# Mixer stage of a two-block transformer kernel: value tiles in halves, gate product in eight pieces, one output block moved

## What is computed

```
u = rmsnorm_2(h, attn_norm_w)
gq, gk, gv, gz, gb, ga, fq, fk, fv, ff = split(u @ w_in)
# gated delta rule, in chunks: M = 16 meta tokens, then 128 and 128
sol = triangular_solve(a_mat + eye, [v * beta, k * (beta * exp(gc))])
v_new = u_c - w_c @ state
o_c = (q_c * exp(g_c)) @ state + qk_c @ v_new
state = state * exp(g_last) + (k_c * exp(g_last - g_c)).T @ v_new
o_gdn = o * rsqrt(mean(o * o) + EPS) * norm_w * silu(gz)
# forgetting attention
p = softmax(causal(q @ k.T * scale + c[q] - c[k]));  o_fox = p @ fv
h = h + concat([o_gdn, o_fox]) @ w_out
h = h + swiglu(rmsnorm_2(h, ffn_norm_w))
```

## Time and profile before

| | us |
|---|---|
| median of 3 runs | 934.2 (932.55 to 935.7) |
| the profiled execution | 935.33 |
| its span in the trace | 933.7 |
| PE busy | 915.9 (98%) |
| DVE busy | 627.7 (67%) |
| ACT busy | 481.6 (52%) |
| granted PE clock, mean | 0.996 of full |

### The profile page before, as it was taken

One profiled execution on the slowest core, in us unless ns is written; L12 is line 12 of the kernel. 1 busy time (PEld: TensorE's weight loads), 2 busy tenths in 40 slices (PEclk: granted clock), 3 DMA queues, 4 the chain that ended last, 5 costly groups with the idle time before them and its releaser, 6 DMA issues.

```text
span 933.7 us, 16660 instructions
## 1 busy us (share of the span) xinstructions
PE 915.9 (98%) x6746; PEld 812.6 (87%) x6746; DVE 627.7 (67%) x962; ACT 481.6 (52%) x845; POOL 98.5 (11%) x107
## 2 busy tenths in 40 slices
PE   8999999999999999999999999999999999999997
PEld 8988778877998999998788789999678899999885
DVE  5974376546896587778874477998665667666543
ACT  6334447436655464565754457665444554445432
POOL 1000031001230000101320003400000011111001
PEclk9999999999999999999999999999999999999999
DMA  9745345555555775332015454432111455555551
GB/s 323 280 161 180 135 151 174 177 180 176 181 189 204 271 259 206 136 136 92 1 57 196 155 184 137 177 136 92 48 47 33 154 203 198 204 181 190 204 193 46
DMA packets 23520, 150.41 MB, mean 161 GB/s; under 512 B 3564, under 2 KB 3848, under 8 KB 6168
## 3 DMA queue, kind: packets, MB, share of 16 engines
q1 hardware_dynamic: 23104, 149.20, 46.3%
q10 hardware_dynamic: 344, 0.18, 0.1%
HBM read 148.30 MB, written 1.05 MB: 160 GB/s over the span
## 4 chain that ended last, share of the span: by engine, by line
PE 81%; DVE 9%; ACT 5%; DMA 2%; issue 2%; POOL 0%; SPq 0%; ACTq 0%; POOLq 0%; DVEq 0%
PE psum L794 77%; DVE ring_parts L2140 4%; DMA ring<-in_weights 2%; ACT high_parts L1688 1%; PE psum L875 1%; ACT R L1877 1%; DVE R L2470 1%; PE psum L1224 1%; DMA h<-in_x 1%; DVE R L2422 1%; PE psum L1569 0%; DVE PTb_parts L2441 0%; DVE PTb L2639 0%; ACT Pf L2060 0%; PE psum L1494 0%
## 5 line engine op out<-in xcount | busy, mean ns | idle before, releaser
L2140 DVE TENSOR_TENSOR ring_parts<-ring,high_parts 128x1024 fp32r<-128x1024 f32 (+1 forms) x272 | 330.1, 1253 | 150.8 <-ACT high_parts L1688 149.6
L1688 ACT CAST high_parts<-ring 128x1024 fp32r<-128x1024 f32 x268 | 268.2, 1051 | 183.0 <-PE psum L794 141.4
L794 PE MATMUL psum<-xT_parts,high_parts 128*128 128x256 f32 (+1 forms) x1024 | 228.3, 284 | 1.5 <-DVE ring_parts L2140 0.7
L794 PE MATMUL psum<-xT_parts,ring_parts 128*128 128x256 f32 (+1 forms) x704 | 197.5, 281 | 0.0
L794 PEld LDWEIGHTS psum<-xT_parts,high_parts 128*128 128x128 f32 x1024 | 172.7, 189 | 3.9 <-issue 1.8
L794 PE MATMUL psum<-high_parts,R_parts 128*128 128x512 f32 (+1 forms) x528 | 164.8, 386 | 0.0
L794 PE MATMUL psum<-R_parts,high_parts 128*128 128x256 f32 x832 | 156.0, 277 | 0.0
L794 PE MATMUL psum<-high_parts,xT_parts 128*128 128x512 f32 x480 | 154.2, 397 | 0.0
L794 PEld LDWEIGHTS psum<-xT_parts,ring_parts 128*128 128x128 f32 x704 | 132.4, 188 | 0.1
L794 PEld LDWEIGHTS psum<-R_parts,high_parts 128*128 128x128 f32 x832 | 130.5, 188 | 0.0
L794 PEld LDWEIGHTS psum<-high_parts,R_parts 128*128 128x128 f32 (+1 forms) x528 | 98.7, 188 | 20.5
(11 more groups left out here) (365 smaller groups left out, 1050.3 us busy)
## 6 DMA issues: line engine op xcount, KB each, us to landing
ring<-in_weights SPq DMA_DIRECT2D x135, 1024.0 KB, 5.0
h<-in_x SPq DMA_DIRECT2D x4, 256.0 KB, 4.5
ring<-in_weights SPq DMA_DIRECT2D x4, 256.0 KB, 5.8
ring<-in_weights SPq DMA_DIRECT2D x2, 512.0 KB, 7.6
G<-in_gains SPq DMA_DIRECT2D x2, 512.0 KB, 6.9
out<-xn SPq DMA_DIRECT2D x2, 512.0 KB, 2.6
R<-in_ret_tabs SPq DMA_DIRECT2D x1, 768.0 KB, 14.5
G<-in_p_t SPq DMA_DIRECT2D x1, 512.0 KB, 6.6
```

The costliest lines, as they stand in the source:

```text
L794: return pe.matmul(out, lhsT, rhs, start=first, stop=last, skip_group_check=True)
L1688: act.copy(as_r(hi), value).then_inc(sem("units_high"), 1)
L2140: return dve.tensor_tensor(as_r(value), value, value_of(hi), ALU.subtract)
```

## The change

It rewrites the list, and the two helpers that cut a tile. Value tile 2 is made in two halves too (`fvh` 2, `fv` 2), with its second half behind Q 2; tile 3's first half moves behind kv 1 and its second half behind kv 0. The gate product was four entries (two halves of k by two token blocks) of 12 matmuls, three of them in levels 1, 2 and 4 and the last one behind Vo 0. It is now eight entries (four quarters of k by two token blocks) of 6 matmuls, seven of them in levels 1 to 5. The output block `mo` 0, 0 moves from behind Vn 2 to ahead of it. The sums and their matmuls are the same.

```diff
-    order += [("fv", 1), ("Q", 1), ("fv", 2), ("Qm", 1), ("Q", 2), ("fvh", 3), ("Qm", 2), ("kv", 1), ("fv", 3), ("kv", 2),
-              ("Fs", 0), ("kv", 0)]
+    order += [("fv", 1), ("Q", 1), ("fvh", 2), ("Qm", 1), ("Q", 2), ("fv", 2), ("Qm", 2), ("kv", 1), ("fvh", 3), ("kv", 2),
+              ("Fs", 0), ("kv", 0), ("fv", 3)]
     beside = {1: ([("vT", 1), ("vT", 2), ("vT", 0), ("Fn", 0)], [("Ft", 0), ("gz", 0, 0)]),
-              2: ([("Fo", 0)], [("Fs", 1), ("gz", 0, 1)]),
-              3: ([("Fn", 1)], [("Ft", 1)]),
-              4: ([("Fo", 1)], [("Fs", 2), ("gz", 1, 0)]),
-              5: ([("Fn", 2)], [("Ft", 2)]),
+              2: ([("Fo", 0), ("gz", 0, 1)], [("Fs", 1), ("gz", 1, 0)]),
+              3: ([("Fn", 1)], [("gz", 1, 1), ("Ft", 1)]),
+              4: ([("Fo", 1), ("gz", 2, 0)], [("Fs", 2), ("gz", 2, 1)]),
+              5: ([("Fn", 2)], [("gz", 3, 0), ("Ft", 2)]),
               6: ([("Fo", 2)], [("Fs", 3)])}
...
-    order += [("W", 1), ("W", 2), ("Fn", 3), ("Vn", 0), ("Ft", 3), ("Vo", 0), ("gz", 1, 1), ("Vn", 1), ("Fo", 3), ("Vo", 1),
-              ("Vg", 1), ("Vn", 2), ("mo", 0, 0), ("Vo", 2), ("Vg", 2), ("H", 0), ("mo", 0, 1), ("mo", 1, 0), ("mo", 1, 1),
+    order += [("W", 1), ("W", 2), ("Fn", 3), ("Vn", 0), ("Ft", 3), ("Vo", 0), ("gz", 3, 1), ("Vn", 1), ("Fo", 3), ("Vo", 1),
+              ("Vg", 1), ("mo", 0, 0), ("Vn", 2), ("Vo", 2), ("Vg", 2), ("H", 0), ("mo", 0, 1), ("mo", 1, 0), ("mo", 1, 1),
               ("H", 1)]
...
-            def rows_input(name, half, n, chunks):
+            def rows_input(name, quarter, n, chunks):
-                if n == 0:
+                if n == 0 and quarter % 2 == 0:
                     unit[name] = next_unit(4)
...
-                for k in range(4):
-                    ins = parts3(product, bank[0:m, :], x_src(4 * half + k, c0, m), w(k, slice(0, 512)),
-                                 half == 0 and k == 0, half == 1 and k == 3)
-                if half:
+                for k in (2 * quarter, 2 * quarter + 1):
+                    ins = parts3(product, bank[0:m, :], x_src(k, c0, m), w(k % 4, slice(0, 512)), k == 0, k == KD - 1)
+                if quarter == 3:
                     main.full(ins, (name, n))
...
-                    channels_input(kind, *key, 4 if (kind, key) == ("fv", [3]) else 0)
+                    channels_input(kind, *key, 4 if kind == "fv" and key[0] > 1 else 0)
...
-                elif kind == "gz" and key[0]:
+                elif kind == "gz" and key[0] == 3:
```

More of the change, by code:

```diff
@@ L1475, in channels_input @@
             def channels_input(name, j, k0=0, k1=KD):
-                if j % 2 == 0:
+                if j % 2 == 0 and k0 == 0:
                     unit[name] = next_unit(KD)
@@ L1502, in rows_input @@
                 c0, m = chunks[n]
-                bank = main.at((name, n)) if half else main.open(pe, (name, n))
-                for k in range(4):
-                    ins = parts3(product, bank[0:m, :], x_src(4 * half + k, c0, m), w(k, slice(0, 512)),
-                                 half == 0 and k == 0, half == 1 and k == 3)
-                if half:
+                bank = main.at((name, n)) if quarter else main.open(pe, (name, n))
+                for k in (2 * quarter, 2 * quarter + 1):
+                    ins = parts3(product, bank[0:m, :], x_src(k, c0, m), w(k % 4, slice(0, 512)), k == 0, k == KD - 1)
+                if quarter == 3:
                     main.full(ins, (name, n))
```

## The result

The changed kernel takes **941.8 us** (median of ten executions, 936.9 to 943.3), the kernel before 933.05 (ten, 932.2 to 937.1): the ratio is 1.0075, with an interval of 1.0058 to 1.0091. By the ratio it is slower by 7 us (5.4 to 8.5), by the medians by 8.8. The forecast was 936.1 with a range up to 938.6 and "within 0.3%" as the likeliest outcome: wrong in both. The profiled execution of after took 941.5 us with a span of 939.9, 6.2 more than before's 933.7.

The account below looks back on a forecast made before the run. The prediction took TensorE (PE), busy 98% of the span, as the bound, leaving only its pauses and clock to gain. A + B2 (B1 within it) + C = +1.9 on 934.2 gave 936.1 us, range 932.0 to 938.6.

Parts of the forecast that it names:

- within 0.3%: Whole kernel: a time that measurement can't tell from no change, 931.4 to 937.0 us; chance 0.65.
- Term A: Values stage: transposes start 1.2 us later behind a 2.75 us pause, at half clock; +1.0 us, ends 0 and +1.35.
- The prediction's own sign of being wrong: Values stage: the forecast is wrong if the value transposes start before 657.3, or level 4's corrections start with their matmuls.
- rival 1: Value transposes: the clock holds there, the rest as forecast, 935.1 us; chance 0.20.
- Term B1: Levels 1 to 3: gate pieces cut waits from 1.2 to about 0.65 us; -0.55 us, ends -1.2 and +0.3.
- Term B2: Levels 4 and 5: two splits delay the corrections, PE idles 2.15 us; +0.9 us with Term B1 counted in.
- The second fall of the clock: Rival: the clock falls again in level 5's 2.15 us pause, costing 1.7 us, 937.8 us; chance 0.20.
- Term C: Output block: the wait moves from Vn 2 to Vo 2, 0.92 us there; 0.0 us, ends -0.9 and +0.3.
- Sum: Step adding 1.0 + 0.9 + 0.0 = +1.9 us to the median of 934.2, giving 936.1 us.

Follow-up runs that it names:

- e15: The changed kernel with three float32 products instead of two in spread_roots(6), same kernel as e9, one profiled execution: 934.9 us.
- e8: The changed kernel with four float32 products instead of two in spread_roots(6), as a control: 942.35 us (one execution).
- e9: The changed kernel with three float32 products instead of two in spread_roots(6): 942.6 us, ratio 1.0084.
- e13: The changed kernel unaltered, run again for one profile: 939.0 us.
- e10: The changed kernel with the output block back behind Vn 2 (value halves and gate pieces only): 937.65 us, ratio 1.0032.
- e7: The kernel before with the output block's move alone and three float32 products instead of two in spread_roots(6): 934.5 us, ratio 1.0012.
- e4: The changed kernel with unread float32 matmuls inserted ahead of SwiGLU gate and up units, at twenty breaks: 945.5 us (one execution).
- e3: The kernel before with the output block's move ahead of Vn 2 alone: 938.5 us, ratio 1.004.
- e11: The changed kernel with the last half of value tile 3 back ahead of Fs 0 and kv 0: 942.7 us (one execution).
- e6: The kernel before with three float32 products instead of two in spread_roots(6): 939.4 us, ratio 1.0065.
- e12: The changed kernel with gate pieces shifted later, so one DVE split in level 4 instead of two: 940.5 us (one execution).
- e16: The changed kernel with three float32 products instead of two in spread_roots(6), same kernel as e15, one profiled execution: 938.3 us.
- e14: The changed kernel unaltered, same as e13, run again for one profile: 946.5 us.

## Why the prediction was wrong

**Term A (+1.0): right for the profiled execution.** Its chain came out as written. ACT, after: the chunk-0 rows and behind them the cast of the last value half; DVE, after: the split and the copies.
```profile
653.53 1.09 ACT L2021 ACTIVATE R<-psum,small 16x128 f32<-16x128 f32 x4
654.53 1.03 ACT L1687 CAST high_parts<-ring 128x1024 fp32r<-128x1024 f32 x1
```
```profile
655.59 1.23 DVE L2139 TENSOR_TENSOR ring_parts<-ring,high_parts 128x1024 fp32r<-128x1024 f32 x1 [2.06 <-ACT high_parts L1687]
```
The pause was forecast at 2.75 us and is 2.88; the half clock at the transposes came. From the mark to the gate block are 36.20 us before (662.22 - 626.02) and 37.09 after (662.10 - 625.01): +0.89. The prediction's own sign of being wrong, transposes before 657.3, has to be read from that mark too: they start at 657.29, but after is 1.01 us ahead, so they come 0.99 later than before. The pause is a matter of the order, the half clock of the execution: e15 has the same pause (2.88 us ahead of 657.26) and a clock of 1.00 from 656 to 664 us, where after has 0.79. That is what rival 1 said of the clock, and there it came.

**Term B1 (-0.55): right mechanism, undersized.** Fo 1 starts 1.11 us earlier than before (681.41 against 682.52), so levels 1 to 3 give 0.99 back. Of the waits that I had left there (0.35 in level 2, 0.15 to 0.2 at Fs 1, 0.1 in level 3) two of 0.17 us stood.

**Term B2 (+0.9): right place and releaser, oversized.** The resumption in level 5 is at 67.51 us from the mark (692.52) against 66.46 (692.48): +1.05, of which A holds 0.89, so B2 is +0.16. The corrections of level 4 were forecast 1.65 us late from two splits; with A taken off they came 0.9 late (685.45 against 684.69, and 1.01 - 0.89 for mark and A). B1's larger gain took up 0.4 of the difference, and ACT's cast began 0.6 us behind the piece's first matmul (683.23 and 682.64) and not 0.9, which is the rest.

**The second fall of the clock: a rival (0.20) that came.** It was priced at 1.7; from the mark to the value product behind the levels after needs 89.99 us and before 87.92, so the part behind level 5 lost 2.07 - 1.05 = 1.0. This too is a draw: e8, e9 and e13 have the same pause of 1.96 or 1.97 us there and a clock of 1.00 from 690 to 704 us.

**Term C (0.0): right in the mixer.** The wait of 0.90 moved from Vn 2 to Vo 2 and is 0.68 (forecast 0.92): 2.07 became 1.89 us at H 0, -0.2.

So the mixer's sum came out at +1.9 us, as forecast, but by luck: 0.9 + 0.2 + 1.0 - 0.2, where a fall of the clock that the forecast left out makes up for what B2 had too much.

**The step that failed** is the one in "Sum": it adds the terms of the mixer to the old time and takes every stage behind for unchanged, because its instructions are. The long stream took 5.5 us more for the same instructions at the same clock, which is neither a term, nor in a rival's price, nor in the range. The trace of before would have warned me: it has streams of the same matmuls at 117.8 ns (20.9 to 54.6 us) and at 113.3 (247.9 to 283.1 us), and its last stream changed from one to the other at `spread_roots(6)`. The two paces were there to be read; I looked at stretches of the mixer only, because PE had no pause behind it.

The medians are 8.8 us apart and the profiles 6.2, because before's profiled execution lies 2.3 us above its median of ten and after's 0.3 below its own. The medians' larger distance fits the half clock: the mean clocks of the changed kernel's ten go from 0.991 to 0.996, and none of them reaches the 0.998 at which the kernel before often runs. e10 agrees, with 3 us for values and gate at the fast pace where the profiles' mixer sum is 1.9. How much of that 3 belongs to the clock wasn't separated further.

No version beat the kernel before. Values alone and gate alone (e1, e2) are at 1.0005 and e7 at 1.0012, all with 1 in the interval: no part gives anything that can be measured, the block's move not even at the fast pace.

## What to carry to other kernels

When a bound engine's stream is long and unbroken, measure its pace per instruction in the old trace and see whether other streams of the same form run at another one: a few per cent of a long stream outweigh every pause in front of it. An edit that loses nothing locally can move such a pace, so a single kernel's time near a half per cent may be luck of the pace, and it is worth comparing the same stretch by instruction counts before a cause is sought in the edit. Filling a pause by moving work ahead of it works only if the moved work's own helpers (here a cast and a split on queues in order) aren't what the next wait is for.

## What the runs showed of the hardware

**Two paces at one clock.** At a granted clock of 1.00 the one-pass matmuls run at 113.3 or 117.8 ns (256 columns) and 228.9 or 233.3 ns (512), 4.4 ns apart in both, and keep it as long as the stream is unbroken (983 matmuls). It changed or stayed at a break by float32 matmuls, by the parity of their number, at all twenty inserted breaks of e4 and at `spread_roots(6)` in all 17 profiles. Two more breaks by two such products are in the same traces. At about 247 us slow became fast in all 17. At about 20.4 us fast became slow seven times and slow became fast five times, but slow stayed slow in five (before, e3, e10, e11, e15). So two products behind a fast stream always made it slow, and behind a slow one mostly fast: the parity rule is a rule of these breaks and not complete, and slow streams differ in something that their pace doesn't show. Two more signs of that: the transposes ahead of 748 us let both paces through, and e6 and e9 turned from slow to fast at the change from 256 to 512 columns, where slow streams behind an even break stayed slow. What in TensorE has this rhythm no run here shows.

The Trainium skill, "TensorE: Matmul & The Clock Gate", section "Back-to-back issue gap", gives one isolated gap for each width at the high clock, columns divided by 2.4 plus 2.5 ns, so an estimate of 109.2 ns for 256 columns and 215.8 for 512. The streams here, in which each matmul has weights of its own (6746 of either on the page), show two values for each width, all above it.

**The clock falls behind short pauses, and not each time.** It fell behind 1.37 us (e12) and behind 1.57 and 0.40 (e11), and held behind 2.88 us in e15 and behind 1.96 or 1.97 in e8, e9 and e13. Of the eight profiles with the changed kernel's mixer (after, e4, e8, e9, e13 to e16) seven have a fall at the value transposes or just behind them and five the one in level 5, with a mean clock from 0.89 (e14, e16) to 0.97 (e8, e13, e15) over the stretch below, though their pauses are equal within 0.02 us. The 64 us of the mixer, columns as in the earlier trace rows, the granted clock being the third number from the end; first e7, then e1, then e10:
```profile
640.00:704.00 64.00, 60.09 (x1015) 49.00 (x1014) 45.10 (x133) 31.70 (x87) 0.00 (x0) 1.00 0.15 52
```
```profile
640.00:704.00 64.00, 59.89 (x957) 47.99 (x955) 41.12 (x120) 29.43 (x76) 0.00 (x0) 0.87 0.15 52
```
```profile
640.00:704.00 64.00, 58.73 (x946) 48.10 (x945) 42.46 (x121) 29.26 (x76) 0.00 (x0) 0.87 0.16 52
```
e7's mixer has the order of before up to the output block, and its clock never fell there; e1's mean of 0.87 is 8 us of clock lost at most. Over the 55 executions of the kernel before that stood beside these runs, the 25 with a mean clock of 0.998 or more have a median of 933.2 us, and the 14 with 0.989 to 0.992 one of 938.2: most of this kernel's scatter is how long the clock stayed down.
